# Hybrid SSD/S5 block on one core: two S5 products on GpSimd, the skip on TensorE, C's decay bank by bank

## The reference

```python
# A: Mamba-2 SSD, 4 groups of 8 heads of 64, state 128, two chunks of 128 tokens
xbc = silu(causal_depthwise_conv(xbc, conv_w, conv_b))        # 4 taps
y_diag = einsum('bcgls,bcgrls,bcsgrp->bclgrp', cb, decay_ls, xdt)
y_off  = einsum('bclgn,bcgrpn,bcgrl->bclgrp', cm, prev, exp(da_cs))
yz = (y_diag + y_off + d_skip * xs) * silu(z); rms per group; @ W_A
# B: S5, 64 groups of 16 channels, 64 complex states each
s = associative_scan(a * s + Bbar u)                          # over the 256 tokens
y = Re(C s) + D * u;  gelu(y) @ W_glu -> glu_a * sigmoid(glu_g)
x = x + g2 * ((sigmoid(gate_a) * A + sigmoid(gate_b) * B) @ W_o)
```

## Time and profile before

| | |
|---|---|
| median of 3 runs | 2483.99 us (2479.97 to 2484.55) |
| the profiled execution | 2477.85 us, span of its instructions 2476.0 us |
| TensorE busy | 2378.0 us, 96% of the span, 15508 matmul records |
| VectorE busy | 1754.9 us, 71%; of it L959 (low parts) 986.4 |
| ScalarE busy | 1052.1 us, 42%; of it L548 (high parts) 803.4 |
| GpSimd busy | 239.8 us, 10% |
| chain that ended last | TensorE 78%, VectorE 14%, DMA 4%, ScalarE 2% |
| mean granted TensorE clock | 0.987 of full |

### The profile page before, as it was taken

The page is one execution under the profiler, slowest core; times in us unless marked ns, Lnnn a source line. Parts: engine busy times, 40 slices in busy tenths (PEclk is TensorE's granted clock), DMA queues, the critical chain, the costliest instruction groups (busy, mean ns, idle before and its releaser), DMA issues.

```text
span 2476.0 us, 38205 instructions
## 1 busy us (share of the span) xinstructions
PE 2378.0 (96%) x15508; PEld 2123.5 (86%) x15508; DVE 1754.9 (71%) x2074; ACT 1052.1 (42%) x1130; POOL 239.8 (10%) x265
## 2 busy tenths in 40 slices
PE   6899999999999999999999999999999999999998
PEld 3488799887899899989889999999788888888987
DVE  3476877778778887988877777787877465444554
ACT  3243333343343454444454444344443444444444
POOL 1421313133133000000000000000000000000000
PEclk9999999999999999999999999999999999999999
DMA  9986877878877875555565457797678556555553
GB/s 358 386 273 244 292 262 259 299 257 295 284 249 273 301 255 191 171 187 173 185 225 176 146 191 268 241 320 273 233 272 301 168 193 200 194 187 174 196 182 112
DMA packets 296991, 584.60 MB, mean 236 GB/s; under 512 B 10324, under 2 KB 35412, under 8 KB 295316
## 3 DMA queue, kind: packets, MB, share of 16 engines
q1 hardware_dynamic: 291408, 559.98, 66.1%
q0 software_dynamic: 4144, 22.28, 2.5%
q10 hardware_dynamic: 1300, 0.35, 0.1%
HBM read 569.98 MB, written 12.58 MB: 235 GB/s over the span
## 4 chain that ended last, share of the span: by engine, by line
PE 78%; DVE 14%; DMA 4%; ACT 2%; issue 2%; SPq 0%; ACTq 0%; DVEq 0%
PE gps L309 73%; DVE wlo L959 6%; PE mps L309 4%; DMA pre<-in_w_ada_dram 4%; DVE acc L977 2%; ACT whi L548 1%; DVE t L1537 1%; PE mps L1835 1%; DVE xz L1084 1%; DVE xw L1229 0%; DVE E L1471 0%; DVE wr L1548 0%; DVE t L1544 0%; DVE wi L1543 0%; DVE wr L1539 0%
## 5 line engine op out<-in xcount | busy, mean ns | idle before, releaser
L959 DVE TENSOR_TENSOR wlo<-raw,whi 128x1024 fp32r<-128x1024 f32 x800 | 986.4, 1274 | 494.0 <-ACT whi L548 491.9
L548 ACT ACTIVATE whi<-raw 128x1024 fp32r<-128x1024 f32 x800 | 803.4, 1052 | 1181.9 <-PE gps L309 1136.1
L309 PE MATMUL gps<-whi,hs 128*128 128x512 f32 (+1 forms) x2816 | 876.1, 388 | 14.5 <-DVE wlo L959 9.8
L309 PEld LDWEIGHTS gps<-whi,hs 128*128 128x128 f32 x2816 | 529.8, 189 | 138.0 <-issue 20.0
L309 PE MATMUL gps<-hs,whi 128*128 128x256 f32 x3072 | 567.5, 287 | 23.0 <-DVE wlo L959 18.4
L309 PE MATMUL gps<-wlo,hs 128*128 128x512 f32 (+1 forms) x1408 | 543.4, 386 | 0.0
L309 PEld LDWEIGHTS gps<-hs,whi 128*128 128x128 f32 x3072 | 483.8, 194 | 34.9 <-DVE wlo L959 20.7
L309 PE MATMUL gps<-ffs,whi 128*128 128x256 f32 (+1 forms) x2064 | 492.9, 322 | 7.5 <-DVE wlo L959 7.5
L309 PE MATMUL gps<-hs,wlo 128*128 128x256 f32 x1536 | 437.2, 285 | 0.0
L309 PE MATMUL gps<-ffs,wlo 128*128 128x256 f32 x1376 | 387.0, 281 | 0.0
L309 PEld LDWEIGHTS gps<-ffs,whi 128*128 128x128 f32 x2064 | 344.6, 191 | 40.2 <-DVE wlo L959 9.5
(11 more groups left out here) (278 smaller groups left out, 1404.6 us busy)
## 6 DMA issues: line engine op xcount, KB each, us to landing
raw<-in_w_ffn_in_dram SPq DMA_DIRECT2D x160, 1024.0 KB
raw<-in_w_ada_dram SPq DMA_DIRECT2D x112, 1024.0 KB
raw<-in_w_in_dram SPq DMA_DIRECT2D x80, 1024.0 KB
raw<-in_w_ffn_out_dram SPq DMA_DIRECT2D x56, 1024.0 KB
pre<-in_w_ada_dram SPq DMA_DIRECT2D x32, 1024.0 KB, 14.4
raw<-in_w_ffn_out_dram SPq DMA_DIRECT2D x40, 768.0 KB
raw<-in_w_b_glu_dram SPq DMA_DIRECT2D x32, 512.0 KB
raw<-in_w_a_proj_dram SPq DMA_DIRECT2D x16, 1024.0 KB
```

What stands on the lines that cost most here:

```text
L309: return pe.matmul(out, lhsT, rhs, start=start, stop=stop, skip_group_check=True)
L548: act.activation(whi[:, mpos % SPLIT, h, :], raw[:, pos % RING, h, :], ACT.Copy).then_inc(hi_ready, 1)
L959: ins = dve.tensor_tensor(wlo[:, mpos % SPLIT, h, :], raw[:, pos % RING, h, :], whi[:, mpos % SPLIT, h, :].bitcast(F32), ALU.subtract)
```

## The change

- S5: L1552 and L1579 leave VectorE and run on GpSimd (`imag_products` and `rot_half` are what it waits for; `rotated` now counts two per cycle, one from each engine, and the wait in front of C_*T2 is `real_turned`). 
- S5: GpSimd scales the identity by D for each tile (`skip`, in the place of `ldt`), and TensorE adds `skip * ub` to C's output in bank 0. L1585 goes; GELU reads PSUM. The next B product waits for GELU. 
- SSD: ScalarE makes `cdec` in two halves, bank 1 ahead of VectorE's differences and bank 0 in the middle of them; VectorE multiplies `cdec` right behind the differences. TensorE takes the `cdec` half of y first and waits for `scores1` behind it, 9 quarters of slabs behind the first half instead of 8, with 6 instead of 7 after it. 
- Phase z: the last six taps of xbc run behind the first low part of z instead of ahead of it. 
- Norms of phases that are not `wide`: the matmul of the squares comes behind slab `slabs - 2` instead of 2 (only the second output phase of the first FFN, with 6 slabs, differs).

```diff
--- before.py
+++ after.py
@@ -134,7 +134,7 @@
 def build(nc, a):
     steps = plan()
     with ExitStack() as ctx:
-        small_base = [0]
+        small_base, base_of = [0], {}
         arena = ctx.enter_context(nc.sbuf_tensor("arena", [P, 53120], F32))
         base = nc.sbuf_base - 53120 * 4
 
@@ -150,7 +150,8 @@
             for s in shape[1:]:
                 size *= s
             size = (size + 31) // 32 * 32
-            t = at(name, 200 * K + small_base[0], shape, dt)
+            base_of[name] = 200 * K + small_base[0]
+            t = at(name, base_of[name], shape, dt)
             small_base[0] += size
             return t
 
@@ -256,7 +257,8 @@
         dcol = small("dcol", [P, NT])
         mag = small("mag", [P, ST])
         hb = small("hb", [P, 4, HEADS])
-        ldt = small("ldt", [P, S5G])
+        skip = small("skip", [P, P])
+        ldt = at("ldt", base_of["skip"], [P, S5G])
         dtv = small("dtv", [P, 2, HEADS])
         da = small("da", [P, 2, HEADS])
         cs = small("cs", [P, 2, HEADS])
@@ -519,10 +521,20 @@
             pool.dma_start(x_kept, xT[:, :, :].rearrange("p t s -> p (t s)")).then_inc(sem("x_saved"), 16)
             pool.wait_ge(sem("h_lo"), 2 * NT)
 
+            for k in range(2):
+                pool.dma_start(tab[:, k], rot_kept[k]).then_inc(sem(f"rot_in{k}"), 16)
+            pool.wait_ge(sem("s5_logdt"), 1)
             for k in range(UT):
-                if k >= 2:
-                    pool.wait_ge(sem("s5_out"), k - 1)
-                pool.dma_start(tab[:, k % 2], rot_kept[k]).then_inc(sem(f"rot_in{k % 2}"), 16)
+                if k:
+                    pool.wait_ge(sem("s5_out"), k)
+                    if k + 1 < UT:
+                        pool.dma_start(tab[:, (k + 1) % 2], rot_kept[k + 1]).then_inc(sem(f"rot_in{(k + 1) % 2}"), 16)
+                pool.tensor_scalar(skip[:, :], ident[:, :], S5_D[:, k:k + 1], None, ALU.mult).then_inc(sem("skip_ready"), 1)
+                pool.wait_ge(sem("imag_products"), k + 1)
+                pool.tensor_tensor(wi[:, :, :], wi[:, :, :], t2[:, :, :], ALU.subtract).then_inc(sem("imag_unrotated"), 1)
+                pool.wait_ge(sem("rot_half"), k + 1)
+                turned = tab[:, k % 2, 1]
+                pool.tensor_tensor(turned, turned, t1[:, :, :], ALU.mult).then_inc(sem("rotated"), 1)
 
             parts = E[0][:, :, :].rearrange("p a b -> p (a b)").rearrange("p (a b) -> p a b", a=4)
             for i in range(GROUPS):
@@ -864,10 +876,14 @@
                     act.wait_ge(sem("seg_in0"), i + 1)
                     act.activation(E[0][:, :, :], E[0][:, :, :], ACT.Exp).then_inc(sem("seg_exp0"), 1)
                     yield
-                    act.wait_ge(sem("seg_in1"), i + 1)
+                    act.wait_ge(sem("seg1"), i + 1)
+                    act.activation(cdec[:, 4:8, :], mps[:, 1, :].rearrange("p (b l) -> p b l", b=4), ACT.Exp
+                                   ).then_inc(sem("row_decays"), 1)
+                    act.wait_ge(sem("seg_in1"), 2 * i + 1)
+                    act.activation(cdec[:, 0:4, :], mps[:, 0, :].rearrange("p (b l) -> p b l", b=4), ACT.Exp
+                                   ).then_inc(sem("row_decays"), 1)
+                    act.wait_ge(sem("seg_in1"), 2 * i + 2)
                     act.activation(E[1][:, :, :], E[1][:, :, :], ACT.Exp).then_inc(sem("seg_exp1"), 1)
-                    act.activation(cdec[:, :, :], mps[:, 0:2, :].rearrange("p a (b l) -> p (a b) l", b=4), ACT.Exp
-                                   ).then_inc(sem("row_decays"), 1)
                     yield
                     yield
                     act.wait_ge(sem("y_gated"), i + 1)
@@ -894,8 +910,8 @@
                 for k in range(UT):
                     for _ in range(6 if k < 3 else 4):
                         yield
-                    act.wait_ge(sem("s5_y"), k + 1)
-                    act.activation(ub[:, k, :], rs[:, :], ACT.Gelu_apprx_tanh).then_inc(sem("s5_gelu"), 1)
+                    act.wait_ge(sem("s5_out"), k + 1)
+                    act.activation(ub[:, k, :], mps[:, 0, 0:S], ACT.Gelu_apprx_tanh).then_inc(sem("s5_gelu"), 1)
                     if k + 1 < UT:
                         yield
 
@@ -1144,10 +1160,11 @@
             def gemm(ph, following, side, after_norm):
                 n0, m0 = starts[id(ph)]
                 per, mper = len(ph.stream), 2 * ph.slabs
-                if later:
+                owed = ph.evac == "silu" and bool(later)
+                if later and not owed:
                     later.pop()()
                 for b in range(2):
-                    if r.q:
+                    if r.q and not owed:
                         dve.wait_ge(psum_free(b), r.q)
                 if r.p:
                     dve.wait_ge(sem("prod_free"), r.p + 1)
@@ -1471,6 +1488,9 @@
                             ins = dve.tensor_scalar(E[c][:, h, :], mps[:, h // 4, P * (h % 4):P * (h % 4) + P],
                                                     cs[:, c, HPG * i + h:HPG * i + h + 1], 0.0,
                                                     ALU.subtract, ALU.min)
+                            if c and h == 3:
+                                ins.then_inc(sem("seg_in1"), 1)
+                                dve.wait_ge(sem("row_decays"), 2 * i + 1)
                         ins.then_inc(sem(f"seg_in{c}"), 1)
 
                     def decay(c):
@@ -1485,12 +1505,12 @@
                     decay(0)
                     yield
                     seg(1)
-                    yield
-                    decay(1)
-                    dve.wait_ge(sem("row_decays"), one)
+                    dve.wait_ge(sem("row_decays"), 2 * one)
                     dve.tensor_tensor(cdec[:, :, :], cdec[:, :, :],
                                       bc[:, GROUPS + i, P:2 * P].unsqueeze(1).broadcast_to([P, HPG, P]), ALU.mult
                                       ).then_inc(sem("c_decayed"), 1)
+                    yield
+                    decay(1)
                     yield
                     dve.wait_ge(sem("y_features"), one)
                     y = E[1][:, :, :].rearrange("p a b -> p (a b)").rearrange("p (a b) -> p a b", a=4)
@@ -1548,8 +1568,6 @@
                     dve.tensor_tensor(WR, WR, T1, ALU.add).then_inc(sem("real_unrotated"), 1)
                     if 5 in stops:
                         yield
-                    dve.wait_ge(sem("imag_products"), one)
-                    dve.tensor_tensor(WI, WI, T2, ALU.subtract).then_inc(sem("imag_unrotated"), 1)
                     dve.wait_ge(sem("real_unrotated"), one)
                     scan(t1, wr, 0)
                     scan(t1, wr, 1)
@@ -1567,7 +1585,7 @@
                     scan(t2, wi, 2)
                     scan(t2, wi, 3).then_inc(sem("imag_scanned"), 1)
                     dve.wait_ge(sem("real_scanned"), one)
-                    dve.tensor_tensor(WR, C_, T1, ALU.mult)
+                    dve.tensor_tensor(WR, C_, T1, ALU.mult).then_inc(sem("real_turned"), 1)
                     if 15 in stops:
                         yield
                     dve.wait_ge(sem("imag_scanned"), one)
@@ -1575,15 +1593,9 @@
                                              ).then_inc(sem("rot_half"), 1)
                     if 16 in stops:
                         yield
-                    dve.wait_ge(sem("rot_half"), one)
-                    dve.tensor_tensor(S_, S_, T1, ALU.mult)
+                    dve.wait_ge(sem("real_turned"), one)
                     dve.tensor_tensor(C_, C_, T2, ALU.mult).then_inc(sem("rotated"), 1)
                     yield
-                    dve.wait_ge(sem("s5_out"), one)
-                    if k:
-                        dve.wait_ge(sem("s5_gelu"), k)
-                    dve.scalar_tensor_tensor(out=rs[:, :], in0=ub[:, k, :], scalar=S5_D[:, k:k + 1],
-                                             in1=mps[:, 0, 0:S], op0=ALU.mult, op1=ALU.add).then_inc(sem("s5_y"), 1)
                     yield
 
             def split():
@@ -1874,7 +1886,7 @@
                                 if ph.evac != "pair" and j < 3:
                                     next(side, None)
                             ins.then_inc(slab_done, 1)
-                            if ph.norm is not None and s == 2 and 2 * i + g > 0:
+                            if ph.norm is not None and s == (2 if ph.wide else ph.slabs - 2) and 2 * i + g > 0:
                                 sum_group(ph.norm, 2 * i + g - 1)
                             if ph.norm == 3 and s == 3 and 2 * i + g > 0:
                                 turn_out(2 * i + g - 1)
@@ -1986,7 +1998,7 @@
                     yield from quarters_of_gates(2 if i else 8)
                     if i == 0:
                         pe.wait_ge(sem("xbc_ready"), 6)
-                        pe.wait_ge(sem("s5_y"), UT)
+                        pe.wait_ge(sem("s5_gelu"), UT)
                     else:
                         pe.wait_ge(sem("y_gated"), i)
```

(15 more changed lines are left out.)

## The result

The changed kernel takes **2485.57 us** (median of 20 runs, 2477.74 to 2490.43), the kernel before 2480.36 beside it (20 runs, 2475.56 to 2485.9). The ratio is **1.0018, 95% interval 1.0009 to 1.0026**: 4.5 us slower, between 2.2 and 6.4. The forecast was 1.4 us faster.

The account below looks back on a forecast made before the run. TensorE, busy 96% of the span, was taken as the bound, so edits win only where it stands still. S5 +13.8 and SSD -15.2 gave -1.4 us: 2476.4 from the profiled execution, 2482.6 on the median's scale, range 2470 to 2493.

Parts of the forecast that it names:

- S5 +13.8: S5 stretch: GpSimd stops, waits at C, skip matmuls and clock dips, less the taps' gain, summed over eight cycles to +13.8 us.
- SSD -15.2: SSD stretch: all four waits for C's decayed copy go (-11.8), with their clock dips (-2.6, -1.3), 0.5 given back: -15.2 us.
- rival (c): S5: full 2.4 us stops, C waiting every cycle, dips at both long gaps; S5 +21, total +6, 2490 us; chance 0.18.
- (a): S5: a long GpSimd instruction does not stop VectorE; S5 -8.2, total -23.4, 2460.6 us; chance 0.12.
- (b): S5: stops fall half into time VectorE waits anyway, no dip added; S5 +8, total -7, 2477 us; chance 0.18.
- The first product on the chain: S5: a product taken from VectorE's chain gives back 1.14 us and costs a 2.1 us stop, net +0.96.
- the second product: S5: starts behind L1574, waits for C_*T2, runs 2.4 us, ends 1.3 later than L1580; C waits 0.15 to 0.2 per clean cycle.
- The skip: S5: D*u as one float32 matmul costs TensorE about 0.4 us, eight times, uncovered.
- The six taps: S5, k = 3: moving six taps behind the low part shortens the gap by 2.4 us and removes a 1.7 us dip.
- rival (d): SSD: gaps close only by half, a low part or decay(1) being the last wait; total +6 to +8, 2491 us; chance 0.08.
- the 0.5 given back: SSD: 0.5 us lost because the sum of squares comes a quarter slab sooner behind the y products.
- The term that was mis-sized: the clock: S5: new gaps of 3.4 and 4.1 us may lower the clock; one and a half dips of 1.7, 2.5 us.

Follow-up runs that it names:

- e4: The changed kernel with both GpSimd products and D*u back on VectorE and GELU from SBUF, leaving C's decay by halves and the taps: 2466.83 us, ratio 0.9936.
- e1: The changed kernel with both GpSimd products back on VectorE, everything else kept: 2469.03 us, ratio 0.9957 to the kernel before.
- e9: e3, with VectorE also waiting for the end of its own C_*T2 before the low parts: 2469.01 us, ratio 0.9949 to the kernel before.
- e3: The changed kernel with only the second product (S_*T1) on GpSimd, WI - T2 back on VectorE: 2487.43 us, ratio 1.0026 to the kernel before.
- e2: The changed kernel with only the first product (WI - T2) on GpSimd, S_*T1 back on VectorE: 2476.66 us, ratio 0.9981 to the kernel before.
- e11: e4 once more, the same kernel, run for an interval of its own: 2465.3 us, ratio 0.9941 to the kernel before.

## Why the prediction was wrong, step by step

**Sign and size.** Forecast: S5 +13.8, SSD -15.2, together -1.4. By the stages of the profile: +20.5, -13.5, and -0.4 behind them. By the time, +4.5. So it came near rival (c), which had +6 and S5 over 20, and for a part of (c)'s reasons: C does wait for GpSimd and the clock does fall, though in other places and by other amounts. The stop itself was 2.2 us (4.55 less 2.35), nearer to the 2.1 of the sum than to (c)'s 2.4. Rivals (a) and (b) fall with the first product: its stops are there, and they lie where TensorE waits.

**Right.** GpSimd's product alone: 2.41 us (forecast 2.4 from 256 and 512 columns). The first product on the chain: idle time +1.0 per clean cycle (0.88 to 1.88) for +0.96. Cycle k = 5, where the second product found a pause, has idle +1.1 for the forecast's 0.96 + 0.15, and k = 7 has +2.1 for 2.1, by luck: 0.6 of it is clock, which the sum did not have there. The skip: clean cycles of 33.2 (e4) against 33.6 (e1), +0.4 each. GELU ahead of the B product cost nothing: among TensorE's waits there is none for it. The six taps took 2.4 us out of k = 3. In SSD the four gaps closed (11.8 us of waits to 0.8, the 0.5 given back being the 0.6 for E) and no gap moved to decay(1) or a low part, so rival (d) falls; its total of 13.5 is 1.7 short of 15.2. A part of the 1.7 is in the size of the dips: TensorE's busy time fell by 3.0 us (267.05 to 264.07) where I had 3.9. Idle time fell by 10.5 (11.85 to 1.33), for the forecast's 11.3.

**The step that failed: the second product "starts behind L1574, waits for C_*T2, runs 2.4 us".** I carried GpSimd's behaviour at a free moment over to the second product without a row of it between operations that follow each other without a pause. There it was passed over by C_*T2 and both low parts and ended 2.2 us later than supposed, so C waited 2.13 and 2.08 us in the clean cycles k = 4 and 6, where the sum had 0.15, and 1.05 in k = 0, where it had none (k = 3's 3.00 is near the 2.6 forecast). e9 is the proof: e3 with a pause of 0.1 us behaves as supposed in the clean cycles (idle 0.8 to 0.9 us, as in e1, where e3 has 2.9 to 3.0) and is 18.4 us faster.

**An error that hid it.** The total idle time came out as forecast: 13.8 less 3.2 of skip and 0.8 of net dips is 9.8, measured 10.2. But two misses of opposite sign lie in it. Too much, by 3.0 us: I charged the first two cycles with 2.1 and 1.8 of idle time and they took 0.8 and 0.1. In k = 1 GpSimd was passed over with the first product too (6.1 us) and stopped a scan behind both low parts, for which nobody waits at once; in k = 0 it was the second. Too little, by 4.0 us: the waits at C in k = 4 and 6. Smaller differences in k = 2 and 7 (-0.6, -0.5) and k = 3 (+0.3) close the account.

**The term that was mis-sized: the clock.** I let a gap cost clock only from about 3 us on, after rows 3, 10 and 11, and counted one and a half new dips less one saved: +0.8 us net. Measured were seven stretches of 3.4 us in S5 where before has the length of three, +7.1 us. This term alone turns -1.4 into +4.9.

The bound of 3 us was a misreading. "Not at one of 2.84" is SSD group 2; group 1 has a gap of 2.84 too, and its grant of 0.57 stands in rows 10 (1360:1364) and was even counted in the sum for C's decay. Group 3 has a gap of 3.08 and a full grant:

```profile
1360.83 0.70 PE L309 MATMUL mps<-cdec,prev 128*64 128x128 f32 x4 [2.84 <-DVE cdec L1491]
...
1477.42 0.77 PE L309 MATMUL mps<-cdec,prev 128*64 128x128 f32 x10 [3.08 <-DVE cdec L1491]
...
1477.00:1481.00 4.00, 3.58 (x46) 3.41 (x47) 3.89 (x6) 0.00 (x0) 0.00 (x0) 1.00 0.64 244
```

So the trace of before showed already that gaps of one length have a dip or have none.

In the kernel after two dips stand at gaps of 3.00 and 2.74 us, five at gaps of 1.87 to 2.08, the size that the stop gives to every clean cycle's gap (0.88 + 1.0). Four more gaps of that size (1.87 to 2.13) had none: that of 1.88 in k = 4 had no dip, that of 1.87 in k = 5 had one. Those of 0.8 to 1.1 had none. All fourteen traces from 930 to 1500 us say the same: none of 85 gaps of 0.7 to 1.6 us has a dip, 25 of 53 of 1.8 to 2.3 us have one, 8 of 10 of 2.5 to 3.1 us, and all 13 over 3.5 us. So for a gap near 2 us half of 1.7 us belonged into the sum. It is not all lost: in k = 5 the dip behind the first product's gap gave VectorE the pause that spared C's wait of 2.1 us. What decides over a single gap is not shown.

**What the change is worth by parts:** by the profiled stages, decay -13.5 us, taps -0.9 to -2.6, skip +3.2, first product +6.1, second +17.2, both +18.6 (15 by the ratios).

## What to carry to other kernels

Before an operation goes to a helper engine, look at what the busy engine does in the very time of it, and in which memory its inputs lie: the same subtraction cost 6 us beside operations on two SBUF tensors and gave 4.5 to 6 us beside operations that read PSUM (in five of the eight cycles). Look at whether the helper gets in at all when the busy engine issues without a pause: a wait of the busy engine on its own last result, costing 0.1 us, was worth 18. And where TensorE is 96% busy, a step that makes a gap of 0.9 us into one of 1.9 costs more than the microsecond, since the clock may fall behind it.

## What was not expected of the hardware

- **Passed over.** GpSimd's product beside back-to-back VectorE operations on two SBUF tensors took 3.3, 5.5, 6.1 or 7.8 us, 2.41 alone. With the first product it got in after one low part, between the two of a pair (k = 3 to 7), with the second not between C_*T2 and the pair nor within it, though the operations follow at the same 0.08 us of overlap; but ahead of the adaLN sum of k = 7 it did get in behind C_*T2. In one and the same place, between L1568 and a low part, it got in in k = 0 and not in k = 1; there the trace shows a difference: the low part of k = 0 started at 953.81, where L1568 ended, that of k = 1 the usual 0.08 us before L1568's end, and e2 has the same pair. What decides where VectorE does not slacken at all stays open; only that a pause of 0.1 us decides for GpSimd is shown, in e9's cycles k = 0 and 3 to 6.
- **VectorE loses less than GpSimd's instruction takes.** It lost 2.2 us beside a product of 2.41, as it had lost 1.08 beside a sum of 1.29: 0.91 and 0.84 of it. Yet the low part that was stopped ended 1.09 us behind the product (1136.81 and 1135.72), and 1.08 behind the sum (700.92 and 699.84), nearly the 1.14 us that it takes of VectorE's time. So it did next to nothing while GpSimd ran, and the loss is smaller because GpSimd began beside the end of the operation ahead (its 2.41 us counted back from its end give 1133.31; the low part ahead ended at 1133.48). By the Trainium skill, page "SBUF — State Buffer", section "Who interferes with whom", the one that comes second is blocked until the whole instruction of the other is over; these rows agree.
- **Half clock behind short gaps.** 3.4 us at 0.50 stood behind gaps of 1.87 to 2.1 us, and e4 and e11, one and the same kernel, differ by 10.3 us of such stretches in S5 (13.7 and 3.4). Their loss by the clock differs by 4.5 us, their idle time by 2.2 the other way, and the stage by 1.7 (321.2 and 319.5). So a difference of one or two us between two profiles of this stage says nothing, and its split into idle time and clock even less.
